# A two-layer decoder trunk: wider expert panels, expert 0 gathered alone, and a tail divided by tiles

## What is computed

```python
def moe_swiglu(x, w_router, w_gate, w_up, w_down):      # x 256 x 1024, 8 experts, 1024 x 3584
    logits = (x @ w_router).astype(jnp.float32)
    top_vals, top_idx = lax.top_k(logits, 2)
    weights = softmax(top_vals)
    combine = sum(one_hot(top_idx, 8) * weights[..., None], axis=-2)
    for e in range(8):
        out += combine[..., e:e + 1] * ((silu(x @ w_gate[e]) * (x @ w_up[e])) @ w_down[e])

h = layer_norm(ALPHA * h + f, ln_g[1, 1], ln_b[1, 1])
h = h + sigmoid(h @ ple_w_gate[1] + ple_b_gate[1]) * (p[1] @ ple_w_proj[1])
```

## Time and profile before

| | us |
|---|---|
| median of 3 runs (lowest, highest) | 1474.14 (1472.51, 1475.07) |
| the profiled execution | 1470.26 |
| its span, first to last instruction | 1468.5 |
| busy in the span: TensorE | 1412.5 (96%) |
| VectorE | 702.5 (48%) |
| ScalarE | 319.8 (22%) |
| GpSimd | 24.6 (2%) |
| moved by DMA | 467.99 MB, mean 319 GB/s |

### The profile page before, as it was taken

The page is one execution under the profiler, slowest core; times in us unless marked ns, Lnnn a source line. Parts: engine busy times, 40 slices in busy tenths (PEclk is TensorE's granted clock), DMA queues, the critical chain, the costliest instruction groups (busy, mean ns, idle before and its releaser), DMA issues.

```text
span 1468.5 us, 27721 instructions
## 1 busy us (share of the span) xinstructions
PE 1412.5 (96%) x12131; PEld 925.5 (63%) x12131; DVE 702.5 (48%) x1128; ACT 319.8 (22%) x432; POOL 24.6 (2%) x51
## 2 busy tenths in 40 slices
PE   8999999999999999999999999999999999999687
PEld 7888788888778877356666664456454454465135
DVE  4795678878874668432332332241422322323247
ACT  4444344344455553000000000000000000000012
POOL 3010000000000000000000000000000000000100
PEclk9999999999999999999999999999999999999998
DMA  9956445555456126999999999999999999999980
GB/s 367 337 197 248 165 172 183 189 200 185 166 177 207 50 78 262 419 412 404 416 414 419 420 419 420 419 418 421 419 419 420 419 420 419 420 420 415 417 348 30
DMA packets 135481, 467.99 MB, mean 319 GB/s; under 512 B 8524, under 2 KB 9376, under 8 KB 134848
## 3 DMA queue, kind: packets, MB, share of 16 engines
q1 hardware_dynamic: 130864, 450.92, 77.9%
q0 software_dynamic: 2992, 12.70, 2.3%
q10 hardware_dynamic: 1504, 2.62, 0.5%
HBM read 462.53 MB, written 3.67 MB: 317 GB/s over the span
## 4 chain that ended last, share of the span: by engine, by line
PE 78%; DMA 13%; DVE 5%; ACT 2%; issue 1%; SPq 1%; POOL 0%; ACTq 0%; POOLq 0%; DVEq 0%
PE ps L1781 76%; DMA ring<-in_moe_w_up_dram 10%; DMA ring<-in_moe_w_down_dram 2%; DMA raw<-in_ple_w_gate_dram 1%; DVE split L1121 1%; PE ps L1799 1%; ACT split L751 1%; DVE h L1169 1%; DVE stats L1173 1%; DVE acc L1164 1%; DVE htl L1136 0%; SPq L578 0%; PE ps L2116 0%; PE ps L2152 0%; DVE acc L1216 0%
## 5 line engine op out<-in xcount | busy, mean ns | idle before, releaser
L1781 PE MATMUL ps<-ring,xt 128*32 128x448 f32 x5632 | 546.2, 542 | 25.9 <-DMA ring<-in_moe_w_up_dram 25.6
L1781 PEld LDWEIGHTS ps<-ring,xt 128*32 128x32 f32 x5632 | 256.7, 110 | 300.0 <-issue 242.1
L1781 PE MATMUL ps<-split,hth 128*128 128x512 f32 x1168 | 366.7, 395 | 6.0 <-DVE htl L1136 2.8
L1699 DVE TENSOR_TENSOR m_hb<-ps,m_sg 128x224 f32<-128x224 f32 x88 | 29.2, 385 | 575.8 <-ACT m_sg L1054 575.8
L1781 PE MATMUL ps<-ring,m_bt 128*32 128x256 f32 (+1 forms) x3472 | 278.4, 469 | 6.8 <-DMA ring<-in_moe_w_down_dram 6.7
L1781 PEld LDWEIGHTS ps<-split,hth 128*128 128x128 f32 x1168 | 218.9, 190 | 53.8 <-DVE htl L1136 3.4
L1781 PEld LDWEIGHTS ps<-ring,m_bt 128*32 128x32 f32 x3472 | 173.0, 110 | 108.7 <-issue 28.8
L1781 PE MATMUL ps<-split,htl 128*128 128x512 f32 x584 | 229.3, 393 | 0.0
L1707 DVE STREAM_TRANSPOSE m_bt<-m_hb 32x224 f32<-32x224 f32 x352 | 205.1, 583 | 5.5
L1054 ACT ACTIVATE m_sg<-ps 128x224 f32<-128x224 f32 x88 | 25.4, 357 | 727.7 <-PE ps L1781 727.7
L1121 DVE TENSOR_TENSOR split<-raw,split 128x2048 fp32r<-128x2048 f32 x52 | 118.7, 2291 | 64.0 <-ACT split L751 63.9
(11 more groups left out here) (256 smaller groups left out, 651.1 us busy)
## 6 DMA issues: line engine op xcount, KB each, us to landing
ring<-in_moe_w_gate_dram SPq DMA_DIRECT2D x128, 896.0 KB, 17.2
ring<-in_moe_w_up_dram SPq DMA_DIRECT2D x128, 896.0 KB, 16.6
ring<-in_moe_w_down_dram SPq DMA_DIRECT2D x128, 896.0 KB, 16.2
raw<-in_gm_w_in_dram SPq DMA_DIRECT2D x14, 1024.0 KB, 14.6
raw<-in_ffn_w_gate_dram SPq DMA_DIRECT2D x14, 1024.0 KB, 5.0
raw<-in_ffn_w_up_dram SPq DMA_DIRECT2D x14, 1024.0 KB, 5.0
raw<-in_ffn_w_down_dram SPq DMA_DIRECT2D x14, 1024.0 KB, 5.0
raw<-in_fox_w_in_dram SPq DMA_DIRECT2D x12, 1024.0 KB, 4.9
```

The source lines that it names most:

```text
L1699: ins = nc.vector.tensor_tensor(m_hb[:, q, :], ps[bank][:, QTR:2 * QTR], m_sg[:, q, :], ALU.mult)
L1781: return nc.tensor.matmul(o, a, b, start=start, stop=stop)
```

## The change

- **Panels.** 1,792 columns in place of 896: 16 blocks, each with 16 loads of gate/up (all eight k of gate first, then the eight of up) and eight of down. A slot now holds one k of one matrix: one run of 7,168 B a partition. The ring keeps its size and its 384 loads. A product still has 448 columns, now all of gate or all of up. Silu of a block starts when its gate is complete. Two narrow blocks stand among the wide ones and two at the end; each is two of the old ones.
- **Buffers.** `m_hb` goes (the product is written over `m_sg`), `m_bt` has one buffer, with an own one for the last block. Silu of a block waits for the transposes of the one before; these wait for the down products of the one before that.
- **Start.** `xh` moves over `acc`, `xl` over the parameters of norm 3. They are made between the steps of the router. Expert 0, which keeps its place, is gathered first: its selector alone, 32 products of 96 columns, two copies, then gate/up of block 0. The other 16 groups are gathered behind that. Loads 13 to 15 wait for the logits only, and the first 16 are issued in the order `FILL`. SP still reads the expert numbers ahead of load 16.
- **End.** All four additions of rows stand behind the last block's transposes. ScalarE applies a Sqrt ahead of the last results. The four remainders of the gate's weights are made by GpSimd (`gate_rest`) into `split1`, which has four places, so that no weight tile waits for another; VectorE makes none. TensorE's gate products and what follows go by tiles: tile 0 whole, then tile 1, each into its own bank; the transposes of tile 1 stand behind three quarters of tile 0.

```diff
-PANEL = 896
+PANEL = 1792
-    SLOT = 2 * PANEL
-    X_BLK = 12
+    SLOT = PANEL
+    X_BLK = 24
-        between = len(few) - (NPAN - 1)
+        between = len(few) - NPAN
+    def gate_banks(b):
+        return (0, 1) if narrow(b) else (0, 1, 4)
+    def up_banks(b):
+        return (6, 7) if narrow(b) else (6, 7, 0)
+    ADD_AT = {len(ORDER) - 1: (0, 1, 2, 3)}
+    FILL = (0, 1, 2, 3, 4, 5, 10, 11, 12, 6, 7, 8, 9, 13, 14, 15)
...
             if end > SPLIT_END[-1]:
-                sp.wait_ge(gx_full, 2 * KD)
+                sp.wait_ge(lg_full, T)
+        for n in FILL:
+            ring_space(n)
             ring_load(n)
+        sp.wait_ge(placed, 1)
+        find_experts()
+        for n in range(RING, N_RING):
+            sp.wait_ge(streams[0]["used"], G_MOE + n - RING + 1)
+            ring_load(n)
...
+        def gate_rest(n):
+            pool.wait_ge(streams[1]["hi"], n + 1)
+            pool.tensor_tensor(split1[:, n, 1], raw[:, n], split1[:, n, 0].bitcast(F32), ALU.subtract)\
+                .then_inc(streams[1]["lo"], 1)
...
+        for n in range(4):
+            gate_rest(n)
...
         small_out(2, 2, NE, slice(0, P))
+        act.wait_ge(s0["h"], H_NORM3 + 2)
+        nc.scalar.copy(xh[:, 0, :], h[:, 0, :]).then_inc(xh_ready, 1)
         tile_hi(1)
+        act.wait_ge(s0["h"], H_NORM3 + 2 * T)
+        nc.scalar.copy(xh[:, 1, :], h[:, 1, :]).then_inc(xh_ready, 1)
         small_out(3, 4, NE, slice(P, S))
...
+                if b or r is not None:
+                    act.wait_ge(bt_ready, hid0 + b)
...
+        nc.scalar.activation(std[:, 0:1], var[:, 0:1], ACT.Sqrt)
         unfold_last()
-        round_hi(0, 1)
-        round_hi(1, 1)
+        gate_hi(0)
         norm_sqrt(1, 0, 1)
+        gate_hi(1)
+        gate_hi(2)
         tile_hi(0, 1)
-        round_hi(2, 1)
         norm_sqrt(1, 1, 1)
+        gate_hi(3)
         tile_hi(1, 1)
...
                 if m > 0 and which == 1:
-                    rest_lo(0, which)
                     stream_lo(0, m - 1, which)
                     stream_lo(1, m - 1, which)
-                    rest_lo(1, which)
...
         for m in range(T):
+            rest_x(0, m)
             dve.wait_ge(lg_full, m + 1)
...
+        select_first(lambda m: slots_e[:, m, 0:1])
...
-        gathered(0)
+        first_gathered(0)
+        select_rest(lambda e, n: slice(e, e + n))
         route_weights()
...
+                if 0 < b < NB - 1:
+                    dve.wait_ge(s0["used"], used0 + (G_MOE + down_at(b - 1) + 8))
...
+        def gather_expert_0(x_at, at_e):
+            for k in range(KD):
+                o = ps[FIRST_BANKS[k // 4]][:, k % 4 * CAP:(k % 4 + 1) * CAP]
+                for x in (xh, xl):
+                    for m in range(T):
+                        last = mm(o, x[:, m, k * P:(k + 1) * P], every[:, m, 0, :], x is xh and m == 0,
+                                  x is xl and m == T - 1)
...
                     gate_up(b)
+                    if b == 0:
+                        pe.wait_ge(route_ready, 1)
+                        gather_rest(at_e, gx0)
```

More of the change, by code:

```diff
@@ L737, in _, with round_hi, gate_hi @@
         s0 = streams[0]
[L739 to L751 removed]
+        def round_hi(g, times=1):
+            slot, ss = g % RAW, g % SPL
+            act.wait_ge(raw_landed[slot], 16 * (g // RAW + 1))
+            if g >= SPL:
+                act.wait_ge(s0["used"], g - SPL + 1)
+            nc.scalar.copy(split[:, ss, 0], raw[:, slot]).then_inc(s0["hi"], times)
+        def gate_hi(n):
+            act.wait_ge(raw_landed2[n], 16)
+            act.wait_ge(s0["used"], used_last(SPLIT1_END[n]))
+            nc.scalar.copy(split1[:, n, 0], raw[:, n]).then_inc(streams[1]["hi"], 1)
         def round_at(gv, gs, rv):
@@ L891, in projected, with ple @@
                     .then_inc(proj_copied, 1)
-        def ple(which, g0, ready, last):
-            st = streams[which]
+        def ple(g0, ready, last):
+            st = streams[0]
             for nb in range(2):
@@ L1114, in seq, with rest_lo @@
             dve.wait_ge(s, step[which])
-        def rest_lo(g, which=0, times=1):
-            slot, ss = place(g, which)
-            st = streams[which]
-            dve.wait_ge(st["hi"], g + 1)
+        def rest_lo(g, times=1):
+            slot, ss = g % RAW, g % SPL
+            dve.wait_ge(s0["hi"], g + 1)
             nc.vector.tensor_tensor(split[:, ss, 1], raw[:, slot], split[:, ss, 0].bitcast(F32), ALU.subtract)\
-                .then_inc(st["lo"], times)
+                .then_inc(s0["lo"], times)
         def rest_at(gv, gs):
@@ L1403, in _, with ple @@
         rest_lo(G_PLE)
-        def ple(which, g0, pp, last):
-            st = streams[which]
-            if which == 1:
-                dve.wait_ge(st["lo"], 2)
+        def ple(g0, pp, last):
+            st = streams[0]
             for nb in range(2):
@@ new lines, in ple @@
+                part = slice(nb * W, (nb + 1) * W)
+                dve.wait_ge(st["used"], g0 + 2 + 2 * nb)
+                for m in range(T):
+                    nc.vector.tensor_tensor(sig[:, m, part], ps[2 * (1 - nb) + m][:, :], ple_b[:, 0, part], ALU.add)\
+                        .then_inc(st["gb"], 1)
+                for m in range(T):
+                    dve.wait_ge(st["gs"], nb * T + m + 1)
+                    seq(nc.vector.tensor_tensor(sig[:, m, part], sig[:, m, part], pp[:, m, part], ALU.mult))
@@ L1445, in ple, with last_ple @@
-                if which == 0:
-                    for m in range(T):
-                        stream_lo(nb, m)
+                for m in range(T):
+                    stream_lo(nb, m)
+        def last_ple():
+            st = streams[1]
+            for m in range(T):
+                for nb in range(2):
+                    pieces = 2 if nb == 1 and m == T - 1 else 1
+                    n = W // pieces
+                    dve.wait_ge(last_gate, 2 * m + nb + 1)
+                    for i in range(pieces):
+                        part = slice(nb * W + i * n, nb * W + (i + 1) * n)
+                        nc.vector.tensor_tensor(sig[:, m, part], ps[GATE_BANKS[2 * m + nb]][:, i * n:(i + 1) * n],
+                                                ple_b[:, 1, part], ALU.add).then_inc(st["gb"], 1)
+                    for i in range(pieces):
+                        part = slice(nb * W + i * n, nb * W + (i + 1) * n)
+                        dve.wait_ge(st["gs"], 2 * m + nb + i + 1)
+                        seq(nc.vector.tensor_tensor(sig[:, m, part], sig[:, m, part], pp1[:, m, part], ALU.mult), 1)
+                        nc.vector.tensor_tensor(h[:, m, part], h[:, m, part], sig[:, m, part], ALU.add)\
+                            .then_inc(st["h"], 1)
@@ L1824, in cols_granules, with cols_by_tile @@
                     between()
[L1826 removed]
+        def cols_by_tile(g, banks, fresh, between=None):
             for m in range(T):
@@ new lines, in gather_rest @@
+        def gather_rest(at_e, gx0):
+            for n in range(2 * KD):
+                half, k = n // KD, n % KD
+                if k == 0:
+                    pe.wait_ge(every_ready, at_e + (half + 1))
+                if n >= 3:
+                    pe.wait_ge((gx_act, gx_dve)[(n - 3) % 2], gx0 + (2 + (n - 3) // 2))
+                e0 = 4 * half if half else 1
+                o = ps[REST_BANKS[n % 3]][:, 0:(4 * half + 4 - e0) * CAP]
+                for x in (xh, xl):
+                    for m in range(T):
+                        one = every[:, m, e0:4 * half + 4, :].rearrange("p e s -> p (e s)")
+                        last = mm(o, x[:, m, k * P:(k + 1) * P], one, x is xh and m == 0, x is xl and m == T - 1)
+                last.then_inc(gx_full, 1)
@@ L2337, in down @@
                 j = ORDER[b][1]
+                bt = m_bt_last if b == NB - 1 else m_bt
                 got = 0
```

392 lines of the change are left out of this document (166 added, 226 removed).

## The result

| | before | after |
|---|---|---|
| median (runs), us | 1474.66 (6) | 1484.04 (6) |
| lowest, highest | 1472.51, 1475.69 | 1480.19, 1484.97 |
| ratio, 95% interval | | 1.0059 [1.0045, 1.0072] |
| the profiled execution, its span | 1470.26, 1468.5 | 1484.01, 1482.2 |
| first expert product | 584.02 | 581.69 |

The changed kernel is slower by 9.4 us; the prediction said 3.6, and its range ended at 1482.5. The last two lines of the table divide the loss of the profiled executions: 4.5 us are there when the ring is through, and the tail adds 9.1.

The account below looks back on a forecast made before the run. TensorE was taken to bound the front and the expert stage until the first narrow block, then the DMA, with VectorE's chain and TensorE's products in the tail. 1474.14 - 2.3 (ring) + 5.9 (tail) = 1477.7 us, range 1463.5 to 1482.5.

Parts of the forecast that it names:

- rest of the gather: Between gate/up of block 0 and block 1: the other 16 groups take 10.0 us, in which no slot is freed.
- a mean slot, DMA-paced: Expert stage where the DMA sets the pace: longer packets bring a slot from 2.231 to 2.203 us.
- a subtraction on GpSimd: Tail, gate remainders: one subtraction of 128 x 2048 taken as two passes, 4.1 us, bounds 2.2 and 9.4.
- first centring: Tail, VectorE's centring of tile 0, held by a GpSimd subtraction: stretched from 0.74 to about 2.1 us.
- the start: Start of the experts: slots_e at 572.3, 32 gather products in 4.2 us, first expert product at 578.0 in place of 584.0.
- The ring's sum: Expert stage: TensorE paces until the first narrow block, then the DMA; 1407.0 before, 1404.7 after, -2.3 us.
- rival D: Port sharing holds in the tail and the packet pair saves 0.064 us a slot: 1473.9 us, no change; chance 0.13.
- The tail's mechanism: Tail: GpSimd's SBUF-reading subtractions and VectorE's instructions with two SBUF inputs exclude each other; the tail gets +5.9 us.
- Rival B: Tail: GpSimd does not hold VectorE, so the tail changes by -6.9 us and the whole takes 1464.9; chance 0.30.
- The price from the Trainium skill: Tail: 4,497 ns for a two-input fp32 GpSimd instruction of 2,048; by it tail +7.5, whole 1479.3 us.
- The slope from two short rows: Tail: AFFINE_SELECT and CAST rows give 0.9 ns a further column, so a GpSimd pass over 2,048 takes 2.0 us.
- rival C: Tail: sharing holds and a GpSimd subtraction takes 5.1 us, a quarter more: +4.0, 1481.7 us; chance 0.13.

Follow-up runs that it names:

- b_warm: The changed kernel with 56 filling products in place of 26 ahead of the wait for member_b; ratio 1.0043 to the kernel before, median 1477.22 us.
- j_x_behind: The changed kernel, remainders on VectorE, xl subtracted behind expert 0's selector, 50 filling products in place of 20 behind the ranks; ratio 0.9981, median 1469.42 us.
- i_warm_both: The changed kernel, GpSimd's subtractions kept, with more filling products ahead of member_b and in two places of the tail; ratio 1.0029, median 1476.25 us.
- a_dve_rest: The changed kernel with its four gate remainders on VectorE again, nothing on GpSimd in the tail; ratio 1.0014 to the kernel before, median 1474.38 us.
- g_before_pool: The kernel before with the first two of its last gate weights' four remainders on GpSimd, not VectorE; ratio 1.0007, tail 49.0 us for 48.3.
- c_two: a_dve_rest with four two-input GpSimd subtractions of 128x2048 on scratch beside the tail, nobody waiting for them; run once, tail 63.7 us.
- e_warm_rest: The changed kernel with the edits of a_dve_rest and b_warm together; ratio 0.9975 to the kernel before, median 1468.01 us beside 1471.88.
- c_one: a_dve_rest with four one-input GpSimd copies of 128x2048 on scratch beside the tail, nobody waiting for them; run once, tail 54.0 us.

## Why the prediction was right or wrong

| term | predicted | measured (after) | with the clock held |
|---|---|---|---|
| slots_e | 572.3 | 572.07 | |
| 32 products of expert 0's gather | 4.2 | 6.85 | 3.5 (b_warm) |
| first expert product | 578.0 | 581.69 | 577.40 (b_warm) |
| 384 products of block 0 | 36.3 | 38.2 | 36.29 (j_x_behind) |
| rest of the gather | 10.0 | 11.05 | 11.04 |
| a mean slot, DMA-paced | 2.203 | 2.211 | |
| last ring products | 1417.95 | 1424.80 | 1418.36 |
| a subtraction on GpSimd | 4.1 | 4.54 | 4.53 |
| first centring | 2.1 | 2.48 | |
| from the last ring products to the end | 54.2 | 57.4 | 53.8 (i_warm_both) |

**The step that failed is the start.** The prediction had the wait in its own numbers: it moved `slots_e` back by 2.9 us and left TensorE's ranks, which stand just ahead of it, with nothing to do for the same time. It did not ask what the clock would do behind that gap, and priced the 32 products of the gather (4.2 us) and the 384 products (36.3) at the full clock. The runs showed 6.85 and 38.2 us. Against the forecast it cost 3.7 us up to the first expert product (4.3 against b_warm, since with the clock held the start is 0.6 better than forecast) and 1.9 on the 384 products. A separate miss of 1.05 us is the rest of the gather, 11.05 for 10.0 at the full clock; 0.85 of it is the wait for the last copy. Together these are 6.7 of the 6.85 us by which the last ring products are late. b_warm and j_x_behind take the gap away by two different means, and both have the predicted 1418 within 0.6 us.

**The ring's sum was right.** From the first expert product to the last ring products the prediction has 840.0 us; b_warm has 841.0, j_x_behind 841.3. TensorE has no wait for the ring up to 1000 us, and the queue moves 424 GB/s behind that. The saving a slot was 0.020 us (2.231 to 2.211), and not the 0.028 of the sum or the 0.043 of rival D.

**The tail's mechanism was right,** and forecast from one row, the gather of 1.93 us, and from the rule that the prediction cites beside it. Rival B is out: VectorE waits in the changed kernel, no longer waits in a_dve_rest, and waits again in g_before_pool and c_two. Its size was off by two terms. A subtraction took 4.54 and not 4.1; four of them are 1.8 us. The price from the Trainium skill (GPSIMD Engine Reference, "3.1 Elementwise") of 4,497 ns is the better one: c_two's took 4.52. The slope from two short rows was a poor base, as the text of rival C said. And TensorE's products behind its waits went at the lower clock: twelve of them from 1461.17, 0.43 us apart in place of 0.23. That is worth some 2.5 us in this profile (12 x 0.2), of the 3.6 by which i_warm_both's tail is shorter. In the other direction the rest of the new tail is better than forecast: with the clock held it is 53.8, not 54.2, though its subtractions are longer.

**The sum over executions.** On the profiled runs the prediction was 1473.9 against 1484.0, 10.1 off (6.85 + 3.25); on the medians 6.3. The difference is the 3.9 us between the profiled execution of before and its median. I put the differences on the median as if before's other executions were the same but for an even stretch. g_before_pool, with the start of before, shows an execution in which the clock fell there, for some 1.3 us, and another 1.6 us came earlier. So that the forecast was nearer on the medians than on the profiles is luck: part of before's 3.9 us may be of the kind that the changed kernel has nearly always. How much of it is not shown.

**What stays open.** Why the clock fell behind the 2.0 us wait, in most executions of the changed kernel and in some of before, where a wait of 2.1 us stands a little later; the runs show when it does, not what decides it. How much of j_x_behind's gain is the order and how much the filling. And what the new panels and the new tail give with the start of before at a full clock: no run has that.

**Where the worth of the change went.** By the two marks: the panels gave some 6 us in the ring; the early start gave 6.6 us with the clock held (577.40 for 584.02) and took 11 back in the gather behind block 0; the clock took 6. So the early start lost 4.4 us even with the clock held, as the prediction's own sum has it (578.0 + 36.3 + 10.0 = 624.3, where the kernel before is through the same 384 products at 620.3); it is no gain that the clock spoiled. The tail's own order gave about 1 us (with the remainders on VectorE 47.0 in four profiles and 48.5 in a_dve_rest, for 48.3), GpSimd's subtractions took some 7, and TensorE's clock behind them some 3.6. With the remainders on VectorE and the clock held at the start, the kernel is 3.9 us faster than the kernel before (e_warm_rest).

## What to carry to other kernels

Before work is moved to an idle engine, look at what both engines read: in these runs a copy or a subtraction of GpSimd, with its inputs in SBUF, held each VectorE instruction with two SBUF inputs that fell on it until it ended, so that a chain of 0.16 us steps turned into one of 4 us steps; a memset held none. When an instruction is put ahead of a chain on one engine, ask which engine will now be idle behind it, and for how long: here TensorE, idle for 2 us between stages, went on at half its clock for some 7 to 14 us in seven profiles of seven; the kernel before idles 2.1 us a little later, and kept the full clock in one profile and lost it for a while in another. And a profile is one execution: where its time lies 4 us from the median, the difference can be such an event, and a sum made on it has to say which of the two kinds of execution it describes.

## What the runs showed of the hardware

- GpSimd, 128x2048 float32: memset 1.81 us, copy 1.89, subtraction with two inputs 4.52 to 4.54. The second input costs 2.6 us more than a copy, which is more than the copy's own time.
- Exclusion runs through the whole instruction, and both engines wait: a 128x1 product waited 4.0 us for one subtraction, got in between two, and the next one waited 4.26 again. Between two copies as well one VectorE instruction got in (the centring that started at 1436.40 in c_one), and the two copies took 4.38 us together for 3.78 alone. In c_two, where each subtraction also waits for the one before, two small products got in (4.15 and 0.16 us).
- VectorE's instructions with one SBUF input, or with one in PSUM and one in SBUF, were not stretched beside GpSimd's subtractions (reciprocal 0.16 at 1434.44, adding the last expert 0.75 at 1430.10).
- The 96-column float32 products of the gather, each with a new weight load, are 0.11 us apart at 2.4 GHz and 0.21 at 1.2 GHz.
